# Gated recurrence of one layer: masked level scores gathered in one matrix per head, one product with the values

## What is computed

```python
def gla_chunk_scan(q, k, v, log_f, s0):      # 4 heads, keys and values 128 wide, chunks of 64 tokens
    def step(s, inp):
        qi, ki, vi, fi = inp
        a = jnp.cumsum(fi, axis=2)
        o_inter = jnp.einsum('bhtd,bhde->bhte', qi * jnp.exp(a), s)
        diff = a[:, :, :, None, :] - a[:, :, None, :, :]
        decay = jnp.exp(jnp.where(tri, diff, NEG_BIG))
        scores = jnp.einsum('bhtd,bhjd,bhtjd->bhtj', qi, ki, decay)
        o_intra = jnp.einsum('bhtj,bhje->bhte', scores, vi)
        a_last = a[:, :, -1, :]
        s_new = (jnp.exp(a_last)[..., None] * s
                 + jnp.einsum('bhjd,bhje->bhde', ki * jnp.exp(a_last[:, :, None, :] - a), vi))
        return s_new, o_inter + o_intra
...
    o_f, s_f = gla_chunk_scan(q, k_f, v, lf_f, s0_f)
    o_b, s_b = gla_chunk_scan(rev(q), rev(k_b), rev(v), rev(lf_b), s0_b)
    o = rms_norm(o_f + rev(o_b), gn) * jax.nn.silu(...)
```

## Times and profile before

| | before |
|---|---|
| median of 3 runs | 2842.94 us (2842.52 to 2843.51) |
| profiled execution, its own time | 2838.66 us |
| its span | 2836.8 us |
| PE / PEld busy | 2741.9 us (97%) / 2225.9 us (78%) |
| DVE busy | 1634.6 us (58%) |
| ACT busy | 1175.8 us (41%) |
| mean granted clock of TensorE | 0.993 of 2.4 GHz |

### The profile page before, as it was taken

One profiled execution on the slowest core, in us unless ns is written; L12 is line 12 of the kernel. 1 busy time (PEld: TensorE's weight loads), 2 busy tenths in 40 slices (PEclk: granted clock), 3 DMA queues, 4 the chain that ended last, 5 costly groups with the idle time before them and its releaser, 6 DMA issues. The chain is left out here.

```text
span 2836.8 us, 36059 instructions
## 1 busy us (share of the span) xinstructions
PE 2741.9 (97%) x14768; PEld 2225.9 (78%) x14768; DVE 1634.6 (58%) x2315; ACT 1175.8 (41%) x1731; POOL 290.8 (10%) x249
## 2 busy tenths in 40 slices
PE   8999999999999999999999999999999999999998
PEld 4888776678878888786687878888786788888886
DVE  5567267675645443567763466653667663566543
ACT  3832434442243333345653443332446553443332
POOL 0110034410001110001200001100003101011100
PEclk9999999999999999999999999999999999999999
DMA  6100210045422323231032122223230231232221
GB/s 261 64 27 1 97 45 31 31 141 187 157 80 93 103 90 104 85 104 45 31 120 102 62 84 95 100 103 103 75 90 16 75 134 45 83 103 97 99 94 59
DMA packets 63220, 249.53 MB, mean 88 GB/s; under 512 B 22352, under 2 KB 24784, under 8 KB 37072
## 3 DMA queue, kind: packets, MB, share of 16 engines
q1 hardware_dynamic: 63056, 247.23, 25.7%
HBM read 245.11 MB, written 2.10 MB: 87 GB/s over the span
## 5 line engine op out<-in xcount | busy, mean ns | idle before, releaser
L309 DVE TENSOR_TENSOR ring_lo<-ring,ring_hi 128x2048 fp32r<-128x2048 f32 x199 | 456.9, 2298 | 507.7 <-ACT ring_hi L302 507.7
L360 PE MATMUL bank<-h_hi,ring_hi 128*128 128x512 f32 x1360 | 539.8, 397 | 6.6 <-PEq L427 3.9
L360 PE MATMUL bank<-h_hi,ring_lo 128*128 128x512 f32 x1360 | 530.3, 390 | 0.0
L302 ACT ACTIVATE ring_hi<-ring 128x2048 fp32r<-128x2048 f32 x199 | 379.3, 1908 | 355.8 <-PE bank L360 318.5
L1700 PE MATMUL bank<-h_hi,ring_hi 128*128 128x512 f32 x960 | 374.3, 390 | 0.0
L1704 PE MATMUL bank<-h_hi,ring_lo 128*128 128x512 f32 x960 | 373.5, 389 | 0.0
L1703 PE MATMUL bank<-h_lo,ring_hi 128*128 128x512 f32 x960 | 373.4, 389 | 0.0
L360 PEld LDWEIGHTS bank<-h_hi,ring_hi 128*128 128x128 f32 x1360 | 255.7, 188 | 62.2 <-issue 8.2
L360 PEld LDWEIGHTS bank<-h_hi,ring_lo 128*128 128x128 f32 x1360 | 255.4, 188 | 54.1
L360 PE MATMUL bank<-h_lo,ring_hi 128*128 128x512 f32 x624 | 243.5, 390 | 0.0
L1700 PEld LDWEIGHTS bank<-h_hi,ring_hi 128*128 128x128 f32 x960 | 180.2, 188 | 37.9 <-issue 0.5
(11 more groups left out here) (480 smaller groups left out, 4806.3 us busy)
## 6 DMA issues: line engine op xcount, KB each, us to landing
ring<-in_stream SPq DMA_DIRECT2D x195, 1024.0 KB, 4.9
mod_w<-in_stream SPq DMA_DIRECT2D x64, 256.0 KB, 3.7
ring<-in_stream SPq DMA_DIRECT2D x7, 512.0 KB, 4.6
ring<-in_stream SPq DMA_DIRECT2D x10, 256.0 KB, 4.1
h_spare<-in_stream SPq DMA_DIRECT2D x2, 1024.0 KB, 9.0
xT<-in_xT SPq DMA_DIRECT2D x2, 1024.0 KB, 18.0
xT<-in_xT SPq DMA_DIRECT2D x1, 2048.0 KB, 9.4
memT<-in_memT SPq DMA_DIRECT2D x2, 1024.0 KB, 5.0
```

Of the source, the lines that this page charges most:

```text
L302: nc.scalar.activation(self.slab_hi(slab + j), self.slab(slab + j), ACT.Copy).then_inc(slab_rounded, 1)
L309: nc.vector.tensor_tensor(lower, self.slab(slab + j), self.slab_hi(slab + j).bitcast(F32), ALU.subtract)\
L360: ins = nc.tensor.matmul(out, lhsT, rhs, start=start and w is w_hi and x is x_hi, stop=stop and w is w_lo)
```

## The change

Level scores and the diagonal of a head now share one matrix of 128 x 512. The diagonal is masked by a product as before, which writes zeros everywhere else; on top of it the levels are written only where they belong, by VectorE with `copy_predicated` for levels 0 to 4 (`BY_DVE` = 5) and by ScalarE for levels 5 and 6 with plain copies of the rows and columns concerned (four instructions of 32 partitions, two of 64). The matrix is multiplied once by the values: `intra(h)` stands for the seven `intra(h, l)` and for `diagonal_sums(h)`. It is issued in the next head, behind level 2. The scores rotate through three banks instead of two, the two matrices alternate by head, and there is one output bank `O` instead of two. ScalarE reads the head before it masks the last level. In the shortened diff the functions come in the order of the file.

```diff
-            BY_DVE = 4
+            BY_DVE = 5
...
-            intra_done = Signal("intra_done0", LEVELS * H)
+            intra_done = Signal("intra_done0", H)
...
-            def scores_of(l):
-                return bank[:, 2 + l % 2, :]
-
-            def O(h):
-                return bank[:, h % 2, :]
+            def scores_of(h, l):
+                return bank[:, 1 + (h * LEVELS + l) % 3, :]
+
+            O = bank[:, 0, :]
+
+            def wait_masked(eng, h, l):
+                if l < BY_DVE:
+                    eng.wait_ge(masked_by_dve.sem, masked_by_dve.at(h * BY_DVE + l + 1))
+                else:
+                    eng.wait_ge(masked_by_act.sem, masked_by_act.at(h * (LEVELS - BY_DVE) + l - BY_DVE + 1))
...
-                def diagonal_sums(h):
...
                 def level(h, l, d):
                     m = 1 << l
                     pe.wait_ge(merged[d].sem, merged[d].at(h * (LEVELS + 1) + l + 1))
-                    if l < 2 and h > 0:
-                        pe.wait_ge(masked_by_act.sem, masked_by_act.at((LEVELS - BY_DVE) * h))
-                    elif 2 <= l < BY_DVE + 2:
-                        pe.wait_ge(masked_by_dve.sem, masked_by_dve.at(h * BY_DVE + l - 1))
-                    elif l >= BY_DVE + 2:
-                        pe.wait_ge(masked_by_act.sem, masked_by_act.at(h * (LEVELS - BY_DVE) + l - 1 - BY_DVE))
+                    if h * LEVELS + l >= 3:
+                        wait_masked(pe, *divmod(h * LEVELS + l - 3, LEVELS))
...
-                def intra(h, l):
...
+                def intra(h):
+                    wait_masked(pe, h, BY_DVE - 1)
+                    wait_masked(pe, h, LEVELS - 1)
+                    if h > 0:
+                        pe.wait_ge(head_read.sem, head_read.at(h))
                     for b in range(TB):
-                        last = nc.tensor.matmul(O(h)[:, b * P:(b + 1) * P], v[:, CB + b, h, :], masked[:, l % 2, b * P:(b + 1) * P],
-                                                start=False, stop=False, skip_group_check=True)
+                        last = nc.tensor.matmul(O[:, b * P:(b + 1) * P], v[:, CB + b, h, :], masked[:, h % 2, b * P:(b + 1) * P],
+                                                start=b == 0, stop=False, skip_group_check=True)
                     last.then_inc(intra_done.sem, 1)
...
-                    diagonal_sums(h)
                     for l in range(LEVELS):
                         if l + 1 < LEVELS:
                             level(h, l + 1, 0)
                             level(h, l + 1, 1)
-                        intra(h, l)
                         if h > 0 and l == 0:
                             update(h - 1, 0)
+                        if h > 0 and l == 1:
+                            intra(h - 1)
...
                 update(H - 1, 0)
+                intra(H - 1)
                 turn(H - 1, 1)
...
                 def mask_diagonal(h):
                     dve.wait_ge(diag_done.sem, diag_done.at(h + 1))
+                    if h >= 2:
+                        dve.wait_ge(intra_done.sem, intra_done.at(h - 1))
...
-                    nc.vector.tensor_tensor(diag.rearrange("p (b n) -> p b n", n=P), diag_bank.rearrange("p (b n) -> p b n", n=P),
+                    nc.vector.tensor_tensor(masked[:, h % 2, :].rearrange("p (b n) -> p b n", n=P), diag_bank.rearrange("p (b n) -> p b n", n=P),
                                             mask, ALU.mult).then_inc(diag_masked.sem, 1)
...
                 def mask(h, l):
-                    if l >= 2 or h > 0:
-                        dve.wait_ge(intra_done.sem, intra_done.at(h * LEVELS + (l - 1 if l >= 2 else 0)))
-                    ones = levels[:, (LEVELS - 1 - l) * P:(LEVELS - l) * P].rearrange("p (o n) -> p o n", o=1).to_broadcast([P, TB, P])
-                    nc.vector.tensor_tensor(masked[:, l % 2, :].rearrange("p (b n) -> p b n", n=P),
-                                            scores_of(l).rearrange("p (b n) -> p b n", n=P), ones, ALU.mult)\
-                        .then_inc(masked_by_dve.sem, 1)
+                    for d in range(DIRS):
+                        dve.wait_ge(level_done[d].sem, level_done[d].at(h * LEVELS + l + 1))
+                    ones = levels[:, (LEVELS - 1 - l) * P:(LEVELS - l) * P].bitcast(I32)
+                    nc.vector.copy_predicated(masked[:, h % 2, :].rearrange("p (b n) -> p b n", n=P),
+                                              ones.rearrange("p (o n) -> p o n", o=1).to_broadcast([P, TB, P]),
+                                              scores_of(h, l).rearrange("p (b n) -> p b n", n=P)).then_inc(masked_by_dve.sem, 1)
...
                 def mask(h, l):
 
                     m = 1 << l
+                    act.wait_ge(masked_by_dve.sem, masked_by_dve.at((h + 1) * BY_DVE))
                     for d in range(DIRS):
                         act.wait_ge(level_done[d].sem, level_done[d].at(h * LEVELS + l + 1))
-                    act.wait_ge(intra_done.sem, intra_done.at(h * LEVELS + l - 1))
                     for g in range(P // m):
...
+                        keys_of, times_of = slice(g * m, (g + 1) * m), slice((g ^ 1) * m, ((g ^ 1) + 1) * m)
+                        last = nc.scalar.activation(masked[keys_of, h % 2, :].rearrange("p (b n) -> p b n", n=P)[:, :, times_of],
+                                                    scores_of(h, l)[keys_of].rearrange("p (b n) -> p b n", n=P)[:, :, times_of], ACT.Copy)
                     last.then_inc(masked_by_act.sem, 1)
...
                     for l in range(BY_DVE, LEVELS):
+                        if h > 0 and l == LEVELS - 1:
+                            read_head(h - 1)
                         mask(h, l)
-                        if h > 0 and l == 5:
-                            read_head(h - 1)
```

More of the change, by code:

```diff
@@ L2212, in scan_branch @@
             levels = work["levels"]
-            queries, decays, masked, diag = work["queries"], work["decays"], work["masked"], work["diag"]
+            queries, decays, masked = work["queries"], work["decays"], work["masked"]
             keys_n, states = work["keys_n"], work["states"]
@@ L2255, in level @@
                     pe.wait_ge(merged[d].sem, merged[d].at(h * (LEVELS + 1) + l + 1))
-                    if l < 2 and h > 0:
-                        pe.wait_ge(masked_by_act.sem, masked_by_act.at((LEVELS - BY_DVE) * h))
-                    elif 2 <= l < BY_DVE + 2:
-                        pe.wait_ge(masked_by_dve.sem, masked_by_dve.at(h * BY_DVE + l - 1))
-                    elif l >= BY_DVE + 2:
-                        pe.wait_ge(masked_by_act.sem, masked_by_act.at(h * (LEVELS - BY_DVE) + l - 1 - BY_DVE))
+                    if h * LEVELS + l >= 3:
+                        wait_masked(pe, *divmod(h * LEVELS + l - 3, LEVELS))
                     for b in range(TB):
-                        last = nc.tensor.matmul(split(scores_of(l)[:, b * P:(b + 1) * P], m)[:, :, t_half[d], :],
+                        last = nc.tensor.matmul(split(scores_of(h, l)[:, b * P:(b + 1) * P], m)[:, :, t_half[d], :],
                                                 keys[d][:, h, CT + b * P:CT + (b + 1) * P],
@@ L2300, in inter @@
                             b = order[d][n] - CB
-                            last = nc.tensor.matmul(O(h)[:, b * P:(b + 1) * P], states[:, d, n, :], queries[:, h % 2, d, b * P:(b + 1) * P],
+                            last = nc.tensor.matmul(O[:, b * P:(b + 1) * P], states[:, d, n, :], queries[:, h % 2, d, b * P:(b + 1) * P],
                                                     start=False, stop=d == 1 and n == NB - 1, skip_group_check=True)
@@ L2404, in mask @@
                     m = 1 << l
+                    act.wait_ge(masked_by_dve.sem, masked_by_dve.at((h + 1) * BY_DVE))
                     for d in range(DIRS):
                         act.wait_ge(level_done[d].sem, level_done[d].at(h * LEVELS + l + 1))
-                    act.wait_ge(intra_done.sem, intra_done.at(h * LEVELS + l - 1))
                     for g in range(P // m):
[L2409 to L2412, removed]
-                                                    ACT.Copy, scale=ones)
+                        keys_of, times_of = slice(g * m, (g + 1) * m), slice((g ^ 1) * m, ((g ^ 1) + 1) * m)
+                        last = nc.scalar.activation(masked[keys_of, h % 2, :].rearrange("p (b n) -> p b n", n=P)[:, :, times_of],
+                                                    scores_of(h, l)[keys_of].rearrange("p (b n) -> p b n", n=P)[:, :, times_of], ACT.Copy)
                     last.then_inc(masked_by_act.sem, 1)
@@ L2417, in read_head @@
                     act.wait_ge(head_done.sem, head_done.at(h + 1))
-                    nc.scalar.activation(y[:, h, :], O(h), ACT.Copy).then_inc(head_read.sem, 1)
+                    nc.scalar.activation(y[:, h, :], O, ACT.Copy).then_inc(head_read.sem, 1)
                 for h in range(H):
@@ L2771, in build_program @@
             work["levels"] = levels
```

(1 more changed line is left out.)

4 lines of the change are left out of this document (removed).

## The result

| | before | after |
|---|---|---|
| median, 16 runs each | 2841.51 us (2836.61 to 2844.68) | 2848.10 us (2843.54 to 2850.53) |
| ratio, 95% interval | | 1.0024 (1.0017 to 1.0031) |
| span of the profiled execution | 2836.8 us | 2846.2 us |
| stage, first VectorE instruction to last read of a head | 125.8 us | 130.7 us |
| heads 0, 1, 2, and 3 with the end | 21.2, 28.5, 29.9, 46.3 | 25.0, 32.6, 29.3, 43.8 |

The account below looks back on a forecast made before the run. TensorE's list bounds the kernel now, VectorE's after the change: gains of 0.2, 3.4, 4.3 and 6.0 us in heads 0 to 3, 13.9, less 1.8 for the clock, 12.1 off 2842.9: 2831 us, range 2820 to 2839.

Parts of the forecast that it names:

- The list of VectorE: VectorE's instructions in a head, rebuilt from their starts: they bound the head after the change, at 25.6 us for 29.9 before.
- The sum: VectorE's terms in head 2 from level 0's merge to the product with the states: 25.6 us; head 1 25.1.
- 111.9 forecast without a drop: Length of the whole stage in us if the clock never falls; 113.7 with the one drop counted.
- head 3 with the end: Last head and the updates behind it: updates start at 27.8 us of the head, gain 6.0; the added product costs nothing.
- The predicated copy: VectorE's masks of levels 0 to 4, twenty on the path: priced like a multiplication of 128 x 512, 0.685 us.
- the second rival: VectorE's predicated copy goes over its 512 columns twice: 10.5 us for 20, gain 3.4, time 2839.5; 10%.
- the fourth: Rival: predicated copy costs as much as the slowest VectorE row of its size, 1.80 us: time 2851; 6%.
- The new waits: Waits of `intra(h-1)`, `mask_diagonal` and ScalarE's masks: nothing, within 0.2 us either way in a head.
- The first rival: TensorE stays the bound and the gain is the whole of what it loses, 25 us: 2818; 6%.
- I count one of the three longer pauses as a drop, for 1.8: TensorE behind level 5 in heads 1 to 3: one pause halves the clock, taking 1.8 us off the 13.9 gain.
- the third rival: All six TensorE pauses in heads 1 to 3 lower the clock: 9.0 us off, gain 4.9, time 2838; 6%.
- the rule of that page on gaps: TensorE's new pauses: idle gaps of such length should do no harm; by it the time would be 2829.

Follow-up runs that it names:

- experiment 7: Changed kernel with direction 0's levels over 128 columns instead of 64 and eight fillers in each of two pauses of heads 1 to 3: 2829.33 us, ratio 0.9950.
- experiment 11: As experiment 7, with six more fillers in the last pause, between head 3's product with the values and its second turn: 2827.15 us, ratio 0.9951.
- experiment 5: Kernel before, with the levels' products with the values over 32 of each block's 128 columns: 2864.77 us, ratio 1.0083.
- experiments 2, 4, 6 and 8: Changed kernel with: two fillers a level, 2835.58 us; direction 0 over 128 columns, 2831.84; fillers in pauses only, 2833.72; direction 0 wide, one filler a level, 2833.46.

## Why the prediction was wrong

**The list of VectorE: right.** The sum gave 25.1 us for head 1 and 25.6 for head 2; experiment 7 has 24.95 and 25.62. Term by term, as predicted and as in the rows of experiment 7: up to level 0's merge 2.6 and 2.68 (220.41 to 223.09), levels 0 and 1 with the recurrence 8.4 and 8.21, level 2 2.7 and 2.76, level 3 2.5 and 2.67, level 4 4.5 and 4.47, level 5 2.1 and 2.15, the rest 2.8 and 2.68. The whole stage: 111.9 forecast without a drop, 110.9 measured. That it comes so close is in part luck: head 0 takes 21.7 us where 20.95 follow from the forecast, since the fifth mask lies in its VectorE list too (0.5 us more from level 4's merge to level 5's), and head 3 with the end takes 38.7 where 40.3 were forecast, since the last updates and products run at full clock, for whose half clock before (290 to 297 us) the forecast made no change. 2831 is near the time of this kernel (2829), not of the one that was changed.

**What each edit was to cost: right.** The predicated copy is priced like the multiplication (0.723 to 0.685), which ends the second rival and the fourth. The Trainium skill (VectorE: DVE Perf Modes, First, the fixed hardware budget) gives the engine two read ports, so that a third stream, the old destination, should have shown in the duration; at 0.04 us more than a multiplication nothing here shows one. The new waits cost nothing that can be seen. The first rival failed as argued: even at full clock the head stays at VectorE's 25.6.

**The clock: the step that failed.** "I count one of the three longer pauses as a drop, for 1.8": the term was 1.8 us and is 19.9, the stage of the changed kernel (130.7) less that of experiment 11 (110.8). Four things were wrong in it. The prediction took pauses as the only cause, since the rows it had, were all of pauses; experiment 5 falls without one, and head 0 of the changed kernel, for which the prediction named no risk, falls after two waits of about 1 us and costs 3.4 us. It let a drop end after two groups; in head 0 it lasted 20.5 us, over all the levels of 64 columns that followed, and with direction 0's levels over 128 columns it didn't come at all (experiment 7). It let both groups behind a pause take 3.6 us instead of 1.8, and then passed on the 1.8 of one of them only. And the third rival, "all six pauses", was priced by the same rule, so that its 9.0 us were not a bound either. A short drop behind a pause comes nearest to what was priced, as at head 2's level 6 in the changed kernel. There the pause is 2.22 us, and from level 5's merge to the next head it took 7.8 us (251.84 to 259.63) where 4.9 were forecast:

```profile
251.84 0.42 DVE L2348 TENSOR_TENSOR ring<-ring,scan_logs 128x256 f32<-128x256 f32 x1
...
252.79 3.68 PE L2256 MATMUL bank<-ring,z 128*128 128x64 f32 x16 [2.22 <-DVE z L2350]
...
259.63 0.69 DVE L2329 TENSOR_TENSOR ring<-cq,xT 128x512 f32<-128x512 f32 x1 [2.16 <-PE bank L2294]
```

2.9 us for one drop, not 1.8: level 6 and the product with the states both ran at half clock. A pause of this length is no sure sign either: the same one before L1445, 2.20 us in both traces, left the clock full before (at 1312 us) and was followed by half clock in the changed kernel (from 1320.6 us on).

What should have been seen before: the products that went were not only time on TensorE's list but 224 of its 512 matmuls over 128 columns, in a stage whose other 448 are of half width behind full loads. The rows of before could not show that the clock depended on them, because there it held; they did show the mixture. The Trainium skill (TensorE: Matmul & The Clock Gate, What's actually happening) states that the throttled state is the default and that activity releases it. The prediction cited the rule of that page on gaps and left this one out. The trace agrees only if activity is not read as the profile's busy time: TensorE was busy for 19.99 of 20 us and its clock stayed at 0.51.

**Outside the stage.** The profiled spans differ by 9.4 us and the stages by 4.9 (the changed kernel's begins 0.2 us earlier, so it ends 4.6 us later). Of the rest, 1.4 us arise in the next stage's first microseconds, where the half clock lasts to about 307 us in the changed kernel (the same instruction of the attention, L1278, starts at 388.51 before and at 394.57 after, 6.1 us apart). The other 3.3 lie behind that instruction, where no instruction was changed; the changed kernel's profile has half clock there from 771, 1321 and 2017 us on, the one before from 1188 and 2010. That this part follows from the change, and not from where a pause happens to fall, isn't shown: the medians are 6.6 us apart, not 9.4.

**What stays open.** How few columns it takes for the clock to fall was not measured, nor were the pauses of heads 1 to 3 filled with narrow products. Fillers that use a free moment without loads of their own were not tried. And experiments 2, 4, 6 and 8 are within each other's intervals.

## What to carry to other kernels

Before taking matrix products off TensorE, look at what is left: if it is mostly products of few columns behind full loads, the clock may fall to half, and the saving with it; give the remaining products more columns where loads hide them anyway (here at no cost, and the other direction writes over the rest), and put fillers of full width where the engine waits. Both together brought the changed kernel from 2848 to 2829 us. A forecast with a clock in it needs the case "it falls and stays down", priced for the whole stage. And a profile in which an engine is busy all the time at half clock is not one where it has too much to do.

## What the runs showed of the hardware that was not expected

- The same loads with fillers of 128 columns ran at a granted clock of 0.99, with fillers of 32 columns at 0.83 over the stage; the kernel before fell from 0.97 to 0.74 (in the slowest execution of four) when its products with the values went from 128 to 32 columns.
- Products over 128 columns instead of 64 cost nothing behind loads of 128 at full clock: the 448 loads of the levels took 192 ns each on average before, and 191 in experiment 7, where half of the products are wide.
- A pause of TensorE of 2.20 us before the same instruction (L1445) left the clock full in one trace and was followed by half clock in another, and in experiment 5 the clock fell with no pause at all.
- `copy_predicated` of 128 x 512 float32 from an accumulation bank under a mask of 32-bit integers took 0.723 us, a multiplication of the same size 0.685.
- A copy by ScalarE over 32 partitions x 128 took 268 ns and over 64 x 256 373 ns, where the masking over all 128 partitions x 64, x 128 and x 256 had taken 329, 367 and 471.
